# A two-layer decoder trunk on one core: identity made on chip, first unit in smaller steps, turns re-dealt

## The reference

```python
x <- x + W_out( mixer(RMSNorm(x)) * silu(z) )        # two layers, x is 256 x 1024 float32
# layer 0, NSA: q, kc, vc, ks, vs, kw, vw, gates, z = split(h @ w_in)
#   rope on q and keys; compressed, selected and window branches, each a masked softmax,
#   summed with sigmoid gates; with 256 tokens all 4 selection blocks are chosen and the window spans all
# layer 1, HGRN2: q, f, i, z = split(h @ w_in); f = lb + (1 - lb) * sigmoid(f); k = 1 - f
#   o_t = sum over s <= t of (q_t . k_s * prod of f between) v_s ; RMS norm per head, times g_norm
return rms_norm(x, final_norm)
```

## Time and profile before

| | |
|---|---|
| time, median of 3 runs | 329.02 us (329.01 to 329.14) |
| span of the profiled execution | 327.3 us |
| outside the span, to the median | 1.7 us |
| PE busy | 316.1 us (97%), 2380 matmuls |
| PE weight loads | 268.5 us (82%) |
| DVE busy | 228.5 us (70%) |
| ACT busy | 188.5 us (58%) |
| POOL busy | 56.8 us (17%) |
| granted TensorE clock, mean | 0.996 |

### The profile page before, as it was taken

The page is one execution under the profiler, slowest core; times in us unless marked ns, Lnnn a source line. Parts: engine busy times, 40 slices in busy tenths (PEclk is TensorE's granted clock), DMA queues, the critical chain, the costliest instruction groups (busy, mean ns, idle before and its releaser), DMA issues.

```text
span 327.3 us, 6178 instructions
## 1 busy us (share of the span) xinstructions
PE 316.1 (97%) x2380; PEld 268.5 (82%) x2380; DVE 228.5 (70%) x408; ACT 188.5 (58%) x400; POOL 56.8 (17%) x55
## 2 busy tenths in 40 slices
PE   8999999998999999999999999999999999998993
PEld 5789778867889887777678878999998788897882
DVE  2788953649659978979838716378359988489824
ACT  4694355347686676758545806838355027898223
POOL 0004022070343333446300000100000011111000
PEclk9999999999999999999999999999999999999998
DMA  7999999806390830043260783663663334002011
GB/s 234 393 326 215 272 358 198 258 36 210 97 209 1 194 67 2 0 131 128 75 248 0 259 299 95 240 228 92 212 241 110 150 112 151 3 0 66 0 64 64
DMA packets 28828, 49.41 MB, mean 151 GB/s; under 512 B 3256, under 2 KB 7744, under 8 KB 28800
## 3 DMA queue, kind: packets, MB, share of 16 engines
q1 hardware_dynamic: 25760, 44.30, 43.3%
q10 hardware_dynamic: 2528, 2.69, 4.1%
q0 software_dynamic: 512, 2.03, 1.9%
HBM read 47.97 MB, written 1.05 MB: 150 GB/s over the span
## 4 chain that ended last, share of the span: by engine, by line
PE 63%; DVE 16%; ACT 8%; issue 2%; POOL 2%; ACTq 0%; DVEq 0%; POOLq 0%
PE bank L553 58%; DVE w_lo L1079 6%; ACT w_hi L832 4%; PE bank L732 3%; POOL rp L1442 1%; DVE nmax L1283 1%; ACT prob L952 1%; PE bank L653 1%; DVE qk L1372 1%; DVE ft L1339 1%; DVE qk L1358 1%; DVE prob_t L1295 1%; PE bank L597 1%; DVE zT L1225 1%; DVE zT L1226 0%
## 5 line engine op out<-in xcount | busy, mean ns | idle before, releaser
L1079 DVE TENSOR_TENSOR w_lo<-raw,w_hi 128x1024 fp32r<-128x1024 f32 (+1 forms) x80 | 89.0, 1155 | 34.5 <-ACT w_hi L832 34.3
L553 PE MATMUL bank<-w_hi,h_hi 128*128 128x512 f32 x192 | 77.4, 409 | 2.0 <-DVE h_lo L1182 1.1
L553 PE MATMUL bank<-w_hi,h_lo 128*128 128x512 f32 x192 | 75.1, 391 | 0.0
L553 PE MATMUL bank<-w_lo,h_hi 128*128 128x512 f32 x192 | 75.1, 391 | 0.0
L832 ACT ACTIVATE w_hi<-raw 128x1024 fp32r<-128x1024 f32 (+1 forms) x80 | 72.9, 967 | 2.1 <-issue 1.9
L553 PE MATMUL bank<-h_hi,w_hi 128*128 128x256 f32 x224 | 64.9, 290 | 0.3 <-DVE vc_lo L1261 0.3
L553 PE MATMUL bank<-h_hi,w_lo 128*128 128x256 f32 x224 | 63.4, 283 | 0.0
L553 PE MATMUL bank<-h_lo,w_hi 128*128 128x256 f32 x224 | 63.3, 283 | 0.0
L553 PEld LDWEIGHTS bank<-w_hi,h_hi 128*128 128x128 f32 x192 | 35.9, 188 | 10.6 <-issue 3.7
L553 PEld LDWEIGHTS bank<-h_hi,w_hi 128*128 128x128 f32 x224 | 42.9, 192 | 1.1 <-DVE vc_lo L1261 0.7
L553 PEld LDWEIGHTS bank<-h_lo,w_hi 128*128 128x128 f32 x224 | 42.9, 192 | 0.2
(11 more groups left out here) (199 smaller groups left out, 424.0 us busy)
## 6 DMA issues: line engine op xcount, KB each, us to landing
raw<-in_hg SPq DMA_DIRECT2D x16, 1024.0 KB, 7.4
raw<-in_nsa SPq DMA_DIRECT2D x12, 1024.0 KB, 8.8
raw<-in_nsa_out SPq DMA_DIRECT2D x8, 512.0 KB, 8.5
raw<-in_hg_out SPq DMA_DIRECT2D x4, 1024.0 KB, 6.6
raw<-in_nsa SPq DMA_DIRECT2D x8, 256.0 KB, 5.7
w<-in_w1k SPq DMA_DIRECT2D x2, 1024.0 KB, 16.1
w<-in_w1v ACTq DMA_DIRECT2D x2, 1024.0 KB, 14.6
x_res<-in_x SPq DMA_DIRECT2D x4, 256.0 KB, 5.1
```

The source lines that it names most:

```text
L553: return nc.tensor.matmul(o, lhsT, rhs, start=start, stop=stop, skip_group_check=True)
L1079: m = V.tensor_tensor(lo, src, hi.bitcast(F32), ALU.subtract)
```

## The change

The identity is no longer loaded. POOL clears it and writes the diagonal, and ACT's queue has one load less in front of the norm weights. SP issues w1 ahead of x(t=1, left). In `HEAD`, the two h pieces of t=0 now stand ahead of w0. The steps of unit 0 now cover one K tile (three matmuls), eight steps for each token tile, and the order of the two low products depends on the token tile. The filler is 2, 1 and 1 matmuls at three places. Both strings are dealt anew, with `SPREAD`, `LAG`, `Z_LAG`, `GATED_LAG` and `CMP_LAG`.

```diff
-IDLE = (5, 1)
+IDLE = (2, 1, 1)
-Z_LAG = 1
+Z_LAG = 2
-ORDER = 'HAHHBAHHBAHHBABCDCCrCDgDDgEEEEggxFFFGkFIIgJgkKKIgIgKKpxLggk...
+ORDER = 'HAHAHHHBAHABBAHBAAABBBBCDCrCCgDDDggEgEEExFFgkFgFKGIKKIIJgkIgKpxppkggq...
-H_ORDER = '...RRRRRRllllzz...
+H_ORDER = '...GRRllRRRRllllzz...
...
     add("idle", 0)
     add("gc", banks=(3,))
+    add("idle", 1)
     add("hT", 0, 0, 0, banks=(4,))
-    add("idle", 1)
+    add("idle", 2)
...
+HEAD[0:4] = HEAD[1:3] + HEAD[0:1] + HEAD[3:4]
+FIRST_LOADS = [("x", 0, 0), ("w", 0), ("w", 1), ("x", 1, 0), ("w", 2), ("w", 3), ("x", 0, 1), ("x", 1, 1),
+               ("w", 4), ("w", 5), ("w", 6), ("w", 7)]
...
-GATED_LAG = 3
-CMP_LAG = 4
+GATED_LAG = 4
+CMP_LAG = 5
...
+                    kk = sl
+                    hi = h_hi[:, kk, t * P:(t + 1) * P]
+                    pe.wait_ge(hi_done, split_count(u, kk))
+                    pe.wait_ge(h0_hi, H_RANK[t, kk])
+                    mm(ps[:], hi, w_hi[:, u, kk], kk == 0, False)
+                    for low in ("h", "w") if t == 0 else ("w", "h"):
+                        if low == "h":
+                            wait_taken(pe, ("hT", 0, t, kk // 2))
+                            m = mm(ps[:], h_lo[:, kk, t * P:(t + 1) * P], w_hi[:, u, kk], False, t == 1 and kk == KT - 1)
+                        else:
+                            parts(u, kk)
+                            m = mm(ps[:], hi, w_lo[:, u, kk], False, t == 0 and kk == KT - 1)
...
-            act.dma_start(ident[:], t_in["ident"]).then_inc(ident_in, 16)
             act.dma_start(g_rows[0:KT], t_in["norm_w"][0].rearrange("(k p) -> k p", p=P)).then_inc(g_cols_in, 16)
...
+            GP.memset(ident[:], 0.0).then_inc(ident_zero, 1)
+            pool.wait_ge(ident_zero, 1)
+            GP.affine_select(ident[:], ident[:], [[-1, P]], ALU.not_equal, 1.0, base=0, channel_multiplier=1).then_inc(ident_in, 1)
             GP.memset(vc_hi[:].bitcast(F32), 0.0).then_inc(zeros, 1)
```

More of the change, by code:

```diff
@@ L75 @@
 RECT_LV = (LAST_LV - 2, LAST_LV - 1)
-ORDER = 'HAHHBAHHBAHHBABCDCCrCDgDDgEEEEggxFFFGkFIIgJgkKKIgIgKKpxLggpkgppqqkgqzsgqzzgszzgatgzsbsszzztstszzvtcszvvvtstsszvtztsvtzastzsvvttsbstvvvtsosovvcotstssvvttssvttsotvtvvovttovvvvoo'
+ORDER = 'HAHAHHHBAHABBAHBAAABBBBCDCrCCgDDDggEgEEExFFgkFgFKGIKKIIJgkIgKpxppkggqpkqggLqsqzszgzzggzagtszszszbszztzstszvtcssvvvttsztvvztsstszzavvttssttbssvvtstovvvvcosstotsstvvstvtovvttottovvvvvoo'
 HT_BANKS = ((4, 5, 6, 7), (0, 1, 4, 5))
-H_ORDER = 'aaaabhhbbbcccchdhddeeeefdfFffFFFFFFQFQQQQQQQGGGGGGRRGGRRRRRRllllzzllllzllllzzllllzzllllzllllzllllzzllllzozzozxzxyyoommmmnyynnnrssrsrrs'
+H_ORDER = 'aaaabbhhbbcccchhdddeeeedfffFfFFFFFQFFQQQQQQGQGGGRGGGRGRRllRRRRllllzzllllzzllllzllzzllllzllllzllllzzlllzlozozxzzxyyoommmmnnyynnrsrrsrss'
 CMP_BANKS = ((1, 1, 7), (7, 6, 1))
@@ L92, in schedule @@
     add("gc", banks=(3,))
+    add("idle", 1)
     add("hT", 0, 0, 0, banks=(4,))
-    add("idle", 1)
+    add("idle", 2)
     nsa = {
-        "A": [(("pa", U_KS, 0, sl), 2) for sl in range(4)],
+        "A": [(("pa", U_KS, 0, sl), 2) for sl in range(KT)],
         "H": [(("hT", 0, t, q), HT_BANKS[t][q]) for q in range(4) for t in range(TT) if (t, q) != (0, 0)],
-        "B": [(("pa", U_KS, 1, sl), 3) for sl in range(4)],
+        "B": [(("pa", U_KS, 1, sl), 3) for sl in range(KT)],
         "C": [(("pb", U_KC, 0, sl), 0) for sl in range(4)],
@@ L341, in program @@
         lo_done = sem("lo_done")
+        ident_zero = sem("ident_zero")
         ident_in = sem("ident_in")
@@ L529, in _ @@
                 if u == 0:
-                    for kk in range(KT):
-                        for t, part in {0: ((0, 0),), 1: ((1, 0),), 4: ((0, 1), (1, 1))}.get(kk, ()):
+                    for what in FIRST_LOADS:
+                        if what[0] == "x":
+                            _, t, part = what
                             half = slice(part * UW, (part + 1) * UW)
                             sp.dma_start(x[:, t, half], t_in["x"][t * P:(t + 1) * P, half]).then_inc(x_in[t][part], 16)
-                        sp.dma_start(dst[:, kk], w[:, kk]).then_inc(first_in[kk], 16)
+                        else:
+                            kk = what[1]
+                            sp.dma_start(dst[:, kk], w[:, kk]).then_inc(first_in[kk], 16)
                     continue
@@ L598, in _ @@
                 elif kind == "gc":
-                    pe.wait_ge(ident_in, 16)
+                    pe.wait_ge(ident_in, 1)
                     pe.wait_ge(g_cols_in, 16)
@@ L1134, in _ @@
             V.memset(flat[HD:P, :, :, :, NC:CS], 0.0).then_inc(flat_zero, 1)
-            dve.wait_ge(ident_in, 16)
+            dve.wait_ge(ident_in, 1)
             V.tensor_tensor(fold[:], ident[:, 0:HD], ident[:, HD:P], ALU.add).then_inc(fold_set, 1)
```

4 lines of the change are left out of this document (2 added, 2 removed).

## The result

| | before | changed |
|---|---|---|
| median | 329.01 us (328.67 to 329.14, 4 runs) | 326.38 us (325.73 to 327.07, 4 runs) |
| span of the profiled execution | 327.3 us | 324.1 us (its time 325.87) |
| PE busy, matmuls (the four fewer are filler passes) | 316.1 us, 2380 | 313.4 us, 2376 |

The ratio is 0.9919, with an interval of 0.9901 to 0.9938. The changed kernel is faster by 2.6 us, where 1.65 were forecast. Its four times lie in two pairs, 325.7 and 325.9, and 326.9 and 327.1; the kernel before has no such gap. The experiments begin with that.

What follows compares the result with a forecast made beforehand. PE was taken to bound the kernel nearly everywhere, leaving the head and some of 3.7 us of waits to win. The terms summed to -1.65 us, 329.02 to 327.4; range 325.7 to 330.2, the forecast's own 326.5 to 328.3.

Steps and rivals of the forecast that it cites:

- Head, -0.2: Start through unit 0: first real matmul at about 7.2 instead of 7.39, unit 0 ending at 20.26; -0.2 us.
- Rival 2: Thinner filler at the start lets TensorE's clock rise later: about +1.2 us, so 328.6 us; chance 0.12.
- Rival 1: Loading POOL's code delays the identity, first real matmul 3.0 us later than 7.39: 330.6 us; chance 0.13.
- `w_lo` at 34: PE's 0.7 us wait for DVE's quarter at 34 shrinks slightly: -0.1 us beside the head.
- `hid`: PE's 0.9 us wait at 74: taken as 0, between -0.9 (covered by two p steps) and +0.8.
- `vc_lo`: PE's 0.3 us wait at 84 goes, with the last compression step earlier and the first z later: -0.3 us.
- Attention, 0: From 90 to 160, no PE wait recorded, only small holes to win or lose: 0, within -1 and +1.5.
- Levels, -0.4: Layer 1's levels, near 256 to 260: five DVE quarters instead of six ahead of the first two-part qk; -0.4 us.
- Outputs, -0.65: Near 297, the 1.1 us h_lo wait shrinks with two ACT quarters instead of three before the square: -0.65 us.
- Rival 3: New waits in the re-dealt middle, hid 0.8 later and 1.1 of holes in attention: 329.3 us; chance 0.20.
- Rival 4: All waits close: hid -0.9, outputs another -0.45, attention -0.3, giving 325.8 us; chance 0.15.

Runs made afterwards that it cites:

- experiment 11: Changed kernel with three filler matmuls in the head's hole, first loads in the earlier kernel's order (x(t=1, left) third, w1 fourth): 325.86 us, ratio 0.9904.
- experiment 2: New head alone, with the deal and lags of the kernel before: 329.96 us (328.23 to 333.80), ratio 1.0027 to the kernel before.
- experiment 3: New deal alone, with the head of the kernel before (identity loaded, 5 and 1 filler matmuls): 326.57 us, ratio 0.9928 to the kernel before.
- experiment 5: New head with three filler matmuls in the hole instead of one, and the old deal: 328.65 us, ratio 0.9989 to the kernel before.
- experiment 4: Changed kernel with three filler matmuls instead of one in the hole behind the first x transposes: 326.00 us, ratio 0.9907 to the kernel before.
- experiment 1: The changed kernel timed again without an edit: 326.85 us (326.04 to 329.60, 10 runs), ratio 0.9938 to the kernel before.
- experiment 10: Changed kernel with three filler matmuls in the hole, identity loaded again instead of made by POOL: 327.53 us, ratio 0.9952 to the kernel before.
- Experiment 6: New head with three filler matmuls in the hole, new deal for layer 0, old for layer 1: 327.47 us, ratio 0.9951 to the kernel before.
- experiment 8: Changed kernel with three filler matmuls in the hole, one z moved ahead of the four l behind the last R: 326.35 us, ratio 0.9921.
- experiment 9: As experiment 8, with the next gate unit's first two quarters put behind the two qk products on DVE: 325.99 us, ratio 0.9907.
- Experiment 12: Changed kernel with three filler matmuls in the hole, only the output letters as before, ACT's quarters in their new places: 326.59 us, ratio 0.9935.
- experiment 7: New head with three filler matmuls in the hole, old deal for layer 0, new for layer 1: 327.49 us, ratio 0.9954 to the kernel before.

## Why the prediction was right, and where it was not

The time lay in the range, and the sign and the cause at large (a busy PE that wins where its waits close) were right; that little but waits could be won was not, as attention shows. The forecast of 1.65 us was 1.0 too small in the medians and 1.5 in the profile, since two terms were too small, one was missing and one had the wrong sign. The measured 326.38 lies just below the forecast's own range (326.5 to 328.3). That it is not further out is in part luck: a late clock in some executions took back what the missing term gave.

- **Head, -0.2: right in path and in the profile, not in the medians.** The first matmul of unit 0 was forecast at 7.2 and came at 7.35, the end of unit 0 at 20.26 and came at 20.29. That x of token tile 1 takes the place of the identity as the gate is shown by the changed profile and by experiment 11. `gc` came at 3.23, not 4.05: the 4 KB of norm weights had landed by then, at most 2.5 us after their issue, where I had given them the 3.3 us of the identity's 64 KB. In the medians the new head with one filler matmul costs 0.9 us with the old deal (experiment 2) and 0.3 with the new one (326.85 against 326.57 of experiment 3, same rounds); with three it gives 0.4 (experiment 5) and 0.6 (experiment 4 against 3). The forecast had left the late clock to a rival. A further 0.29 us, a hole at 21.04 in the kernel before that is in no list of waits, went with the new head; I had not seen it. Experiment 3, which has the old head, has it still, between its last two rows here:

```profile
20.89 0.28 PE L553 MATMUL bank<-h_lo,w_hi 128*128 128x256 f32 x1
21.01 0.28 PE L553 MATMUL bank<-h_hi,w_lo 128*128 128x256 f32 x1
21.34 0.38 PE L553 MATMUL bank<-h_hi,w_hi 128*128 128x256 f32 x1
```

- **Rival 2, the late clock: it is there in part of the executions**, beside the forecast and not instead of it. I had priced it at 1.2; two more filler matmuls are worth 1.3 between medians with the old deal and 0.85 with the new. The one profile of the changed list that shows it, experiment 1, lost 0.44 at the head, with x 0.8 earlier. Its condition was half right: PE does stand still before x, but not before `gc`, which runs at 3.23 while the filler runs to 3.30. And the hole alone does not decide: to 5.2 us PE did the same in the changed kernel's two profiles, with the rise at 5.2 in one and at 10.2 in the other. The Trainium skill (TensorE: Matmul & The Clock Gate, What's actually happening) says that sustained activity lifts the clock; the rows of experiments 1, 4 and 10 agree.
- **Rival 1, POOL's code: out.** The diagonal took 0.29 us at 1.18, behind a wait of 0.24 for the memset. The 6 us of the Trainium skill (GPSIMD Engine Reference, Instruction dispatch) do not show for this operation here.
- **`w_lo` at 34, -0.1; `hid`, 0; `vc_lo`, -0.3.** They went from 0.7, 0.9 and 0.3 to 0.15, to 0.36 for `w_lo` at 72.6 and 0.29 for `hid` at 74.6, and to nothing. That is -1.1 of waits, against -0.4. The stage as a whole gained 0.7, since holes of other kinds grew. For `hid` I had chosen the middle of a range of -0.9 to +0.8; the two `p` steps covered more than ACT's longer queue cost.
- **Attention, 0: wrong, the missing term, -0.9.** I looked for waits there, and there are none in either kernel. Fewer and longer runs of one kind of step account for 0.2 of it (last section); the other 0.7 lies in small holes between and within other kinds of steps. Experiment 6 has the gain with layer 0's deal, but none of mine changed one cause alone, so it stays open.
- **Levels, -0.4: wrong, +0.2 by the waits.** By the measure of the table PE neither won nor lost there (+0.05 between 236 and 275). The waits for DVE's `qk` (0.7) went, as worked out. But the new string puts two `l` ahead of the last four `R`, so the next four `l` stand right behind the `R` whose result they need, through ACT: 0.89 us. I had counted letters and not asked what the first of them waits for. Experiments 8 and 9 show that neither order of this stage that I tried is worth more than about 0.1.
- **Outputs, -0.65: mis-sized, -1.13.** I let ACT gain 0.5 with the square held by its own queue. ACT's two squares came 2.4 and 3.3 us earlier and the end of PE's output matmuls only 1.8, so `h_lo` overtook PE: both its halves, which the next matmul needs, are done at 295.04, 0.4 us before that matmul starts. Experiment 12 puts over half of it on the letters, which I had counted as covered by ACT's queue.
- **0.26 us near 190**, in no list of waits, went with layer 1's deal (experiments 6 and 7). I have no cause for it.
- **Rival 3: out.** The wait for `hid` fell, the new one for `w_lo` at 72.6 is 0.36, and attention gained. **Rival 4, 325.8: nearer than the forecast.** It had `hid` at -0.9 (it was -0.6), the outputs 0.45 further (they were) and attention at -0.3 (it was -0.9), but not the loss at the levels nor the late clock.

What stays open: executions of experiment 2 above 331 us are longer than a late clock explains (0.44 us at the head in experiment 1, 1.3 between medians), and none of them was profiled. Within the head, the order of `HEAD` and the steps of one K tile were not varied by themselves.

## What to carry to other kernels

When a wait at the start goes away, ask what lands next and what TensorE does until then: if it stands still, give it filler that ends before the landing, and look at several executions, since one profile may show only the good kind. Here two more filler matmuls made the changed kernel 0.85 us faster than it was in the same rounds (326.00 against 326.85). Against that, the old load order (325.86) and experiment 9 (325.99) cannot be told apart. Where PE has no waits, add up the rows of each kind of step before and after; where it has, ask of each moved letter what it needs, not only how many letters stand before it.

## What the runs showed of the hardware

**A run of matmuls of one kind has a fixed cost beside its matmuls.** In attention, the products with the values (4 matmuls a step) take, from their first start to the next step's, 0.58 to 0.59 us for one step, 1.01 for two and 1.44 for three. A step more costs 0.43, so a run costs 0.15 on top. Before, a run of four steps keeps to this too (1.88). First before, then changed:

```profile
150.91 0.65 PE L553 MATMUL bank<-prob_t,v_tok 128*64 128x256 f32 x4
151.50 0.50 PE L553 MATMUL bank<-p_ct,vc_hi 128*128 128x512 f32 x1
```

```profile
114.36 1.52 PE L561 MATMUL bank<-prob_t,v_tok 128*64 128x256 f32 x12
115.80 0.50 PE L561 MATMUL bank<-p_ct,vc_hi 128*128 128x512 f32 x1
...
159.62 2.62 PE L561 MATMUL bank<-prob_t,v_tok 128*64 128x256 f32 x20
162.17 0.50 PE L561 MATMUL bank<-p_ct,vc_hi 128*128 128x512 f32 x1
```

The kernel before has 13 such runs there and the changed one 10, which by this sum would be 0.45 us of the 0.9. It is less: the last run shown, five steps, takes 2.55 us where the sum gives 2.31, and one of four takes 2.02. All runs of this kind together take 12.45 us before and 12.26 in the changed kernel, 0.2 less. No list of waits shows any of it.

**The landing of a large load varied by 2 us from profile to profile.** The two loads of w1k (1024 KB each) took 15.4 to 17.5 us in the fourteen profiles, and 15.8 and 17.3 in the two of the changed kernel. PE comes to them just as they land: there is no wait up to 16.5 us, and one of 0.3 to 1.1 from 16.7 on.

**The page's row of granted clock shows 1.0 before the clock has risen.** The spacing of the matmuls tells it: 0.43 against 0.23 us for 512 columns.
